# A second copy of the rotary keys on partitions 64 to 127 for the middle query tile, and the latent heads' normalisation ahead of a low part

## The reference, cut to what matters

```python
q = rmsnorm(q, q_g)                      # over 128 + 64 features of a head
k = rmsnorm(k, k_g)
q = concat([q[..., :128], apply_rope(q[..., 128:], cos, sin)])
k = concat([k[..., :128], apply_rope(k[..., 128:], cos, sin)])
s = einsum('bqhd,bkhd->bhqk', q, k) * scale      # 192 features: 128 plain and 64 rotary
out = einsum('bhqk,bkhd->bqhd', softmax(s), v)
```

## Time and profile before

| | |
|---|---|
| median of 3 runs | 2786.84 us (2786.68 to 2787.22) |
| the profiled execution | 2787.14 us, of it the span from first to last instruction 2785.5 us |
| granted TensorE clock | 0.999 of full speed |
| PE busy | 2769.1 us, 99% of the span |
| DVE busy | 1651.7 us, 59% |
| ACT busy | 1248.0 us, 45% |
| DMA | mean 179 GB/s |

### The profile page before, as it was taken

The page is one execution under the profiler, slowest core; times in us unless marked ns, Lnnn a source line. Parts: engine busy times, 40 slices in busy tenths (PEclk is TensorE's granted clock), DMA queues, the critical chain, the costliest instruction groups (busy, mean ns, idle before and its releaser), DMA issues.

```text
span 2785.5 us, 58122 instructions
## 1 busy us (share of the span) xinstructions
PE 2769.1 (99%) x22890; PEld 2739.7 (98%) x22890; DVE 1651.7 (59%) x2215; ACT 1248.0 (45%) x1553; POOL 83.1 (3%) x123
## 2 busy tenths in 40 slices
PE   9999999999999999999999999999999999999998
PEld 9999999999999999999999999999999999999998
DVE  7667786666666454455555665555655555554444
ACT  6456654434343444433444554444443334444443
POOL 0000000000000000000111400000000000000000
PEclk9999999999999999999999999999999999999999
DMA  7433445555455555555554455555555555555555
GB/s 245 141 131 113 142 160 193 187 178 192 171 196 174 193 178 196 186 186 181 181 178 165 160 172 184 188 183 186 185 186 185 186 183 181 181 182 196 188 180 176
DMA packets 138876, 497.83 MB, mean 179 GB/s; under 512 B 16544, under 2 KB 17056, under 8 KB 138752
## 3 DMA queue, kind: packets, MB, share of 16 engines
q1 hardware_dynamic: 135728, 491.34, 51.5%
q0 software_dynamic: 3024, 4.66, 0.9%
HBM read 493.31 MB, written 2.62 MB: 178 GB/s over the span
## 4 chain that ended last, share of the span: by engine, by line
PE 97%; DVE 1%; ACT 1%; issue 0%; DMA 0%; DVEq 0%; ACTq 0%; SPq 0%
PE acc L1326 31%; PE acc L1328 31%; PE acc L1327 31%; DVE wlo L817 1%; PE aux L1379 1%; PE aux L1460 0%; PE aux L1462 0%; PE aux L1359 0%; ACT whi L461 0%; PE aux L1370 0%; PE aux L1468 0%; PE aux L1454 0%; PE aux L1385 0%; DMA raw<-in_wts 0%; PE aux L1575 0%
## 5 line engine op out<-in xcount | busy, mean ns | idle before, releaser
L817 DVE TENSOR_TENSOR wlo<-raw,whi 128x1024 fp32r<-128x1024 f32 x926 | 1121.5, 1228 | 810.8 <-ACT whi L461 807.3
L1326 PE MATMUL acc<-xh,whi 128*128 128x256 f32 (+3 forms) x4968 | 1411.0, 284 | 1.6 <-DVE wlo L817 1.0
L1328 PE MATMUL acc<-xh,wlo 128*128 128x256 f32 (+3 forms) x4968 | 1399.1, 282 | 0.0
L1327 PE MATMUL acc<-xl,whi 128*128 128x256 f32 (+3 forms) x4968 | 1396.3, 281 | 0.0
L461 ACT ACTIVATE whi<-raw 128x1024 fp32r<-128x1024 f32 x926 | 958.2, 1055 | 889.3 <-PE acc L1328 876.4
L1326 PEld LDWEIGHTS acc<-xh,whi 128*128 128x128 f32 (+1 forms) x4968 | 937.3, 189 | 7.4 <-issue 4.9
L1327 PEld LDWEIGHTS acc<-xl,whi 128*128 128x128 f32 (+1 forms) x4968 | 934.7, 188 | 0.4
L1328 PEld LDWEIGHTS acc<-xh,wlo 128*128 128x128 f32 (+1 forms) x4968 | 934.7, 188 | 0.0
L1326 PE MATMUL acc<-acth,whi 128*128 128x256 f32 x1408 | 395.6, 281 | 0.0
L1328 PE MATMUL acc<-acth,wlo 128*128 128x256 f32 x1408 | 395.6, 281 | 0.0
L1327 PE MATMUL acc<-actl,whi 128*128 128x256 f32 x1408 | 395.6, 281 | 0.0
(11 more groups left out here) (293 smaller groups left out, 2277.6 us busy)
## 6 DMA issues: line engine op xcount, KB each, us to landing
raw<-in_wts SPq DMA_DIRECT2D x928, 512.0 KB, 4.1
bias<-distances POOLq DMA_DIRECT2D x64, 32.0 KB, 3.4
bias<-in_na_bias POOLq DMA_DIRECT2D x8, 217.7 KB, 3.0
h<-in_hT SPq DMA_DIRECT2D x3, 544.0 KB, 4.5
out_T<-result SPq DMA_DIRECT2D x3, 384.0 KB, 2.8
h<-in_hT SPq DMA_DIRECT2D x2, 272.0 KB, 4.1
distances<-quads POOLq DMA_DIRECT2D x1, 512.0 KB, 12.5
out_T<-result SPq DMA_DIRECT2D x1, 512.0 KB, 2.7
```

Source lines behind the costliest of these rows:

```text
L817: dve.tensor_tensor(wlo[:, slot_of(at, j), :], raw[:, slot_of(at, j), :], whi[:, slot_of(at, j), :].bitcast(F32), ALU.subtract).then_inc(l ...
L1326: pe.matmul(dst, hi, x_hi(kt), start=kt == 0, stop=False)
L1327: pe.matmul(dst, hi, x_lo(kt), start=False, stop=False)
L1328: last = pe.matmul(dst, lo, x_hi(kt), start=False, stop=kt == chunks * per_chunk - 1)
```

## The change

There are two edits. First, `qr` and `kr` get 128 partitions in place of 64. DVE writes the rotary keys twice, to partitions 0 to 63 and 64 to 127, and the middle query tile's 86 columns of `qr` to partitions 64 to 127 as well. PE takes the middle tile (`t = 1`) from the upper half. Second, in step 1 DVE's `mla_normed(hd)` moves ahead of `low_part(AT_QKV, j)`.

```diff
-        qr = at("qr", T0 + 4352, [ROPE, L])
-        kr = at("kr", T0 + 5440, [ROPE, L])
+        qr = at("qr", T0 + 4352, [P, L])
+        kr = at("kr", T0 + 5440, [P, L])
...
-                dve.tensor_tensor(kr[:], kpe, sq2[0:ROPE, 1, :], ALU.mult)
+                for half in (slice(0, ROPE), slice(ROPE, P)):
+                    dve.tensor_tensor(kr[half], kpe, sq2[0:ROPE, 1, :], ALU.mult)
                 dve.drain()
-                dve.tensor_tensor(qr[:, 0:NQ], sqr[:, Q0:L], sq2[0:ROPE, 0, Q0:L], ALU.mult)\
+                dve.tensor_tensor(qr[ROPE:P, QR:2 * QR], sqr[:, Q0 + QR:Q0 + 2 * QR], sq2[0:ROPE, 0, Q0 + QR:Q0 + 2 * QR], ALU.mult)
+                dve.tensor_tensor(qr[0:ROPE, 0:NQ], sqr[:, Q0:L], sq2[0:ROPE, 0, Q0:L], ALU.mult)\
                     .then_inc(MLA.s["qk"], 1)
...
                     evict_group()
+                    mla_normed(hd)
                     low_part(AT_QKV, j)
-                    mla_normed(hd)
...
                 for t in range(QT):
-                    last = pe.matmul(aux[0:QR, t, 0:L], qr[:, t * QR:(t + 1) * QR], kr[:], start=False, stop=True)
+                    half = slice(0, ROPE) if t % 2 == 0 else slice(ROPE, P)
+                    last = pe.matmul(aux[0:QR, t, 0:L], qr[half, t * QR:(t + 1) * QR], kr[half], start=False, stop=True)
                 last.then_inc(MLA.s["scores"], 1)
```

## The result

| | before | changed |
|---|---|---|
| median of 16 runs each | 2786.68 us (2786.06 to 2788.02) | 2780.95 us (2779.97 to 2782.01) |
| span of the profiled execution | 2785.5 us | 2779.6 us |
| granted TensorE clock | 0.999 | 0.999 |

The change makes the kernel 5.73 us faster: ratio 0.9979, 95% interval 0.9973 to 0.9986. I had forecast 2782.1 us in a range from 2780.9 to 2785.6: the measured time lies at the very low end of the range, the gain of 5.7 us is more than the forecast 4.7, and it just passes the 5.6 us that I had taken for the bound of a visible change, to which I gave a chance of 0.21. The change is clear of no change at all, but the interval reaches to both sides of that bound of 0.2%.

What follows compares the result with a forecast made beforehand. PE's own work was taken as the bound, 97% of the chain that ended last. Overlap 3.0 us plus 1.7 us from fewer waits and slower starts made 4.7 us off the 2786.84 us median: 2782.1 us, range 2780.9 to 2785.6.

Steps and rivals of the forecast that it cites:

- I take 0.38 us per head: Rotary scores on PE: gain from overlapping the two halves, between loads hidden (0.46) and exposed (0.32); 3.0 us over eight heads.
- The price of the copies: DVE, each head: the second key copy and the 86 query columns add 0.50 us, bounds 0.34 and 0.85 us.
- the likeliest case: Whole kernel: the time stays within 0.2%, 5.6 us, of before; chance 0.77.
- waits in front of the plain scores: PE ahead of the plain latent scores: waits gone in heads 0, 1, 4, 6, 7 (2.02 us), head 5's 0.50 us longer.
- slower starts behind waits: Plain latent scores on PE: 0.04 us slower behind a wait; five waits gone save 0.20 us.
- The upper end: Rotary scores with weight loads hidden: next chunk at 1.07 in place of 1.53 us, 0.46 us per head, 3.7 us.
- The bound of 0.85: DVE copies per head with both added instructions at full duration, 0.43 and 0.42 us: 0.85 us.
- the prediction's own sign of being wrong: Wrong if the plain latent scores still wait in heads 1 or 4, or a chunk in steps 3 or 4 waits for a low part.
- The first: Rotary scores: the halves don't overlap, only the moved normalisation gains; 2785.1 us, chance 0.25.
- the third: Rotary scores: each change of half costs 0.16 us, no overlap; 0.9 us slower than before, 2787.7 us, chance 0.05.
- The second: Rotary and plain scores: full overlap, hidden loads, all five waits gone; 5.4 us off, 2781.5 us, chance about 0.22.
- The fourth: DVE: normalisation held by ACT's inverse root, no idle time filled; 1.7 us gain in all, 2785.1 us, chance 0.04.

Runs made afterwards that it cites:

- edit 1 alone: Kernel before plus the upper-half copies and the middle rotary tile taken from the upper half, low part still ahead of the normalisation: 2787.98 us, ratio 1.0004.
- edit 2 alone: Kernel before with only the normalisation moved ahead of the low part, no copies, all rotary scores on partitions 0 to 63: 2784.42 us, ratio 0.999.
- the low part behind the maxima: Changed kernel, but in heads 4 to 7 step 1's low part is made behind the neighbourhood maxima of step 2: 2780.36 us, ratio 0.9976.

## Why the prediction was off

Its mechanism was right in nearly every part; two terms of its sum failed. The overlap was put at 3.0 us by the step "I take 0.38 us per head", and it measured 0.46 us in every head, 3.7 us in all. And the stretches behind the heads were taken as unchanged, a term put at nothing without a reason, where some 0.6 us were gained. The price of the copies, 0.50 us where they take 0.70, was off the other way and hid 0.2 us of that. So the likeliest case, a gain too small to be told (0.77), didn't come about. The terms, against 5.9 us between the spans and 5.73 us between the medians (0.1 us more lies ahead of the heads, and 0.1 us is lost between them):

| term | forecast, us | measured, us |
|---|---|---|
| overlap of the halves | 3.0 | 3.7 |
| waits in front of the plain scores | 2.0 - 0.5 = 1.5 | 1.3 |
| slower starts behind waits | 0.2 | 0.3 |
| output projections (DVE's stalls) | none | 0.6 |

- **The overlap.** The step "I take 0.38 us per head, the middle of the first two" was the largest miss: 0.7 us. (The middle of 0.46 and 0.32 is 0.39, which makes 3.1 and changes nothing.) The upper end, 0.46 us, is what every head shows, and taking the overlap back costs the same 3.7 us. What the middle allowed for, a weight load of the other half laid bare at each change of half, doesn't occur: two loads start at 96.52 together, and the pairs start 0.01 us apart. The Trainium skill ("TensorE: Matmul & The Clock Gate", Part 3) says this of tiles on different rows, about 4 ns apart and loads pulled ahead; I had weighed it and taken the middle instead, because the trace contradicts the same passage on loads for the same rows. On different rows the trace agrees with it.
- **The order of starts.** I had assumed that matmuls start in program order, each waiting only for the one before it on its own half. That the result was 1.07 us all the same was luck, for it came by another course: the pairs are the lower half's first two with the upper half's two. The same passage of the Trainium skill also has matmuls starting in program order; the run with the order 0, 2, 1 contradicts it, with 1.07 us in place of 1.30.
- **The copies.** Priced at 0.50 us, they take 0.70. The bound of 0.85 held. I had read the 0.08 us by which one instruction starts before the end of the last from L954 and applied it to instructions that change the half they write. But from the first `kr` to the second (92.33 to 92.77) and from L955 to L956 (93.28 to 93.53) the full duration passes. The trace of before had a nearer pair, which I didn't use: L928 and L929 each write another group of partitions, and the second starts 0.44 us behind the first, whose duration is 0.43:

```profile
89.80 0.43 DVE L928 TENSOR_TENSOR sqr<-qg,tab 32x272 f32<-32x272 f32 x1
90.24 0.43 DVE L929 TENSOR_TENSOR sqr<-qg,tab 32x272 f32<-32x272 f32 x1
```

  Whether the change of output partitions or something else in these instructions is the cause, no run here separates.
- **The waits.** Gone in heads 0, 4, 6 and 7, all but 0.04 us in head 1, and grown in head 5 from 0.89 to 1.58 us, where I had said 1.39. This is the copies' price again, and the 0.04 us is, strictly, the prediction's own sign of being wrong (a wait left in head 1). Head 4, with 0.13 us to spare and copies that took 0.20 more, just escapes: its idle time is 0.08 us longer than shown, since the next instruction can start 0.08 us before the record in front of it ends. So the maxima came 1.30 + 0.08 - 0.70 = 0.68 us sooner, and the wait was 0.67. Its plain scores still show most of the slower start (192.37 to 193.90, 1.53 us).
- **The 0.6 us in the output projections.** I had looked for side effects only in the turns of the heads, and took every stretch behind them as unchanged. The trace of before has DVE's idle time for issue in it, but nothing there says that it would go. It is the term that carried the result past the bound: without it the median would be some 2781.5 us, an estimate.
- **Rivals.** The first (no overlap, 2785.1 us) and the third (a change of half priced like a change of height) fall: both end at 1.53 us or more for the rotary scores. The second, full overlap and the waits gone, was named at 2781.5 us with 0.22 and is what came about in the heads, but for 0.2 us of waits left in heads 1 and 5; that the median lies below it is the output projections' doing. The fourth falls, since the normalisation starts as soon as DVE is free (91.52).

The chance for "faster" was too low also because the whole upper end of the overlap lay within 0.2 us of the bound, so that a term of half a microsecond anywhere decided the verdict.

## What to carry to other kernels

Small products over 64 rows can be put on the two halves of the array and run side by side even in plain float32 and in either of the two program orders tried, and one copy of an operand buys nearly a third of the time of three such products (1.53 to 1.07 us). But the copy is paid on the engine that makes it, so look first for idle time ahead of that engine's work and move the copy into it: here the copies alone lost time, and paid only with the new order. Where a gain is of the size of a few stalls, compare the stretches that the change doesn't touch: here 16 more instructions ahead of them were worth half a microsecond by themselves.

## What the runs showed of the hardware

- Two matmuls on different halves of the rows start 0.01 us apart and stream at full pace beside each other, each 0.23 us for 272 float32 columns, with their weight loads starting together.
- A half's matmuls can start ahead of earlier ones of the other half (order 0, 2, 1: 1.07 us, as in order 0, 1, 2; the last in program order started 0.45 us before the last of all). Its signal still came behind all of them: DVE started on the scores 1.20 us behind the first, against 1.18 us in order 0, 1, 2.
- DVE instructions that write another half of the partitions than the one before took their full duration to the next start (0.44 and 0.25 us), where L954 and L956 let the next start 0.08 us before their end. The cause isn't shown.
- A DVE loop stalled up to 0.44 us for issue in kernels with one number of instructions ahead of it and not with 16 more, and of three reductions ahead of it the second came 0.2 us late; PE lost some 0.6 us by both.
- Left open: between 1660 and 2041 us, where PE has no wait, the profiles of edit 1 alone, edit 2 alone and the low part behind the maxima have 847 to 849 matmuls in 100 us and the others that were counted 845 to 846, with the granted clock at 1.00 in all. It makes these three spans about 0.9 us shorter, and doesn't go with any edit: of the nine runs with the low part behind the maxima two took 2779.0 and 2779.1 us and the others 2780.2 to 2780.6, and the profiled one is of the two.
- Single executions differ at their start as well: the chunk's last matmul ahead of head 0's scores, where no edit has reached PE yet, starts between 94.07 us (the changed kernel again) and 95.22 us (edit 1 alone). So the spans of two single executions say little below a microsecond, and the stretches compared above say more.
- A balanced split, in which the third tile's keys would be shared by both halves, wasn't tried.
